# Gate and decay rows copied to all partitions by DMA, and the rotary embedding's turned halves read across partitions by VectorE, in a two-layer trunk kernel

## The reference, cut to what matters

```python
def _rotary(a, pos):                       # layer 0, on the retention's q and k
    ang = pos[:, None] * inv[None, :]      # inv: 64 frequencies
    cos, sin = jnp.cos(ang), jnp.sin(ang)
    a1, a2 = a[..., :half], a[..., half:]  # the halves of a head's 128 channels
    return jnp.concatenate([a1 * cos - a2 * sin, a1 * sin + a2 * cos], -1)

def _mlstm_step(carry, inp):               # layer 0
    b = jnp.cumsum(lf, axis=-1)
    logw = jnp.where(_causal(c), b[..., :, None] - b[..., None, :] + it[..., None, :], -jnp.inf)
    m_t = jnp.maximum(b + m[..., None], logw.max(-1))
    w = jnp.exp(logw - m_t[..., None])
    carry_scale = jnp.exp(b + m[..., None] - m_t)
    ...

def _gdn_step(S, inp):                     # layer 1
    gc = jnp.cumsum(g, axis=-1)
    G = gc[..., :, None] - gc[..., None, :]
    A = beta[..., :, None] * jnp.einsum('bhtd,bhsd->bhts', k, k) * dec_strict   # exp(G), masked
    o = jnp.exp(gc)[..., None] * jnp.einsum('bhtd,bhde->bhte', q, S) + ...
```

## Time and profile before

| | |
|---|---|
| median of 3 runs | 1496.48 us (1495.94 to 1501.11) |
| profiled execution, its own time | 1487.38 us |
| its span, first to last instruction | 1485.6 us |
| TensorE busy | 1404.6 us (95%) |
| VectorE busy | 996.4 us (67%) |
| ScalarE busy | 723.0 us (49%) |
| GpSimd busy | 256.8 us (17%) |
| mean granted TensorE clock | 0.969 of full speed |

### The profile page before, as it was taken

How to read it: one execution, slowest core, us unless ns; L and a number is a source line. 1 busy time by engine, 2 the same in 40 slices (tenths; PEclk the granted TensorE clock), 3 DMA queues, 4 the chain that set the end, 5 groups by cost and what they waited for, 6 DMA issues and landing times.

```text
span 1485.6 us, 18615 instructions
## 1 busy us (share of the span) xinstructions
PE 1404.6 (95%) x8014; PEld 1202.4 (81%) x8014; DVE 996.4 (67%) x948; ACT 723.0 (49%) x608; POOL 256.8 (17%) x166
## 2 busy tenths in 40 slices
PE   7999997999999989999998897999999999999994
PEld 6898886799999788997667566888888888888882
DVE  4533466654454578662866756878888888888886
ACT  3434312433333467311221434767777677677771
POOL 0110303000000001000421040000000004356771
PEclk9999998999999999999798987999999999999997
DMA  6532732646443133212245275999999993400003
GB/s 248 162 102 86 238 100 77 222 141 192 145 132 114 39 98 102 80 54 58 66 140 183 83 266 219 370 384 382 380 371 392 385 377 141 170 15 15 16 15 101
DMA packets 80890, 254.81 MB, mean 172 GB/s; under 512 B 11568, under 2 KB 47700, under 8 KB 68008
## 3 DMA queue, kind: packets, MB, share of 16 engines
q1 hardware_dynamic: 66008, 224.53, 41.7%
q0 software_dynamic: 14800, 29.10, 6.4%
HBM read 306.09 MB, written 16.70 MB: 217 GB/s over the span
## 4 chain that ended last, share of the span: by engine, by line
PE 77%; DVE 11%; DMA 5%; ACT 4%; issue 3%; POOL 0%; POOLq 0%; SPq 0%; DVEq 0%; ACTq 0%
PE PS L615 11%; PE PS L617 10%; PE PS L616 10%; PE PS L1321 7%; PE PS L1319 7%; PE PS L1324 7%; DMA u_raw<-in_w_moe 4%; PE PS L595 3%; PE PS L1342 3%; PE PS L1346 3%; PE PS L1343 3%; PE PS L1021 2%; ACT u_hi L1735 1%; PE PS L733 1%; PE PS L739 1%
## 5 line engine op out<-in xcount | busy, mean ns | idle before, releaser
L2598 DVE TENSOR_TENSOR u_lo<-u_raw,u_hi 128x2816 fp32r<-128x2816 f32 x144 | 442.9, 3090 | 106.8 <-ACT u_hi L1735 106.5
L1735 ACT ACTIVATE u_hi<-u_raw 128x2816 fp32r<-128x2816 f32 x144 | 368.1, 2562 | 163.9 <-DMA u_raw<-in_w_moe 113.6
L615 PE MATMUL PS<-x_in_hi,p_hi 128*128 128x304 f32 x480 | 155.5, 324 | 10.7 <-DVE x_in_lo L1978 10.7
L1319 PE MATMUL PS<-u_hi,xg_hi 128*128 128x512 f32 x576 | 141.6, 378 | 4.9 <-DVE xg_lo L2680 2.5
L617 PE MATMUL PS<-x_in_hi,p_lo 128*128 128x304 f32 x480 | 146.2, 305 | 0.0
L616 PE MATMUL PS<-x_in_lo,p_hi 128*128 128x304 f32 x480 | 146.2, 305 | 0.0
L1321 PE MATMUL PS<-u_hi,xg_lo 128*128 128x512 f32 x576 | 142.5, 380 | 0.0
L1924 POOL DMA_INDIRECT u_raw<-in_w_moe,wpick x48 | 125.4, 2612 | 90.5 <-PE PS L1324 66.4
L1324 PE MATMUL PS<-u_lo,xg_hi 128*128 128x512 f32 x576 | 140.9, 377 | 0.0
L615 PE MATMUL PS<-x_out_hi,w_parts 128*128 128x304 f32 x416 | 127.5, 306 | 7.0 <-DVE x_out_lo L1978 7.0
L617 PE MATMUL PS<-x_out_hi,w_parts 128*128 128x304 f32 x416 | 126.5, 304 | 0.0
(11 more groups left out here) (536 smaller groups left out, 2496.7 us busy)
## 6 DMA issues: line engine op xcount, KB each, us to landing
u_raw<-in_w_moe SPq DMA_DIRECT2D x96, 1408.0 KB, 8.3
p_raw<-in_w_first SPq DMA_DIRECT2D x40, 512.0 KB, 3.5
p_raw<-in_w_second SPq DMA_DIRECT2D x28, 512.0 KB, 3.5
dring<-in_ffn_w_down SPq DMA_DIRECT2D x8, 1408.0 KB, 7.4
wring<-in_ffn_w_gate SPq DMA_DIRECT2D x9, 1024.0 KB, 5.6
wring<-in_ffn_w_up SPq DMA_DIRECT2D x9, 1024.0 KB, 8.7
wring<-in_w_out SPq DMA_DIRECT2D x2, 2048.0 KB, 7.9
o_rows<-zT POOLq DMA_DIRECT2D x6, 512.0 KB, 6.8
```

What stands on the lines that cost most here:

```text
L615: mm(out, w[0], x[0], start=start, stop=False)
L1319: mm(PSf[:, a:a + w], x_hi, w_hi[:, a:a + w], start=k == 0, stop=False)
L1735: A(uhi[n % HIS][:], uraw[n % RAW][:], COPY).then_inc(s("u_hi"), 1)
L2598: TT(ulo[n % RAW][:], uraw[n % RAW][:], uhi[n % HIS][:].bitcast(F32), SUB).then_inc(s("u_lo"), 1)
```

## The change

**Rows.** The products `decays`, `carries` and those for `GROW[2]` and `GROW[0]` are gone. POOL stores the rows into a small DRAM tensor `row_copies`, waits for the store, and loads them back to all 128 partitions with a stride of zero: `ROW[4]` as three loads into the parts of `wm`, `ROW[6]` into `ebc`, `GROW[2]` into `qe` and `decI`, `GROW[0]` into `kb`, and the block ends into `dbc`. VectorE's `m_ex` now takes two heads in one instruction, from `wm` itself, and stands in iterations 9 and 10 in place of 7 and 8. ScalarE no longer copies `ebc`, and takes `exp` of `qe` in place. `decI` gets its mask with one addition.

**Rotary embedding.** `rotate` and its matrix are gone. `turn` is two VectorE instructions over 64 partitions each, in which the input comes from the other 64 partitions. POOL's `cos` multiply, which overwrites `turn`'s input, now waits for it (`rotm`). In POOL's program the store and the three loads of `ROW[4]` stand ahead of both multiplies, and the store of `ROW[6]` between them.

```diff
+        rowd = nc.dram_tensor("row_copies", [4, 4, 344], F32, kind="Internal").ap()
...
@@ TensorE, layer 0 @@
             for n in range(1, 6):
                 unit0(n)
-            rotate(0)
             unit0(6)
             pe.wait_ge(*at("ld_cc", 16))
+            unit0(7)
+            unit0(8)
+            unit0(9)
+            unit0(10)
             pe.wait_ge(*at("m_rows", 1))
-            decays(0, 4, at("m_rows", 1))
-            decays(1, 5, at("small_ev", 1))
-            unit0(7)
-            decays(2, 4, at("m_ex", 1))
-            decays(3, 5, at("m_ex", 2))
-            unit0(8)
             pe.wait_ge(*at("m_exp", 1))
-            carries(0, 4, at("m_ex", 3))
-            carries(1, 5, at("m_ex", 4))
-            unit0(9)
-            rotate(1)
-            carries(2, 4, at("m_ebc", 1))
-            carries(3, 5, at("m_ebc", 2))
-            unit0(10)
-            pe.wait_ge(*at("m_ebc", 3))
...
             unit0(12)
             pe.wait_ge(*at("a_ev", 12))
-            pe.wait_ge(*at("rotm", 2))
             pe.wait_ge(*at("m_col", 1))
-            pe.wait_ge(*at("m_ebc", 4))
+            pe.wait_ge(*at("small_ev", 1))
...
@@ TensorE, layer 1 @@
-                if n == 4:
-                    pe.wait_ge(*at("g_col", 1))
-                    pe.wait_ge(*at("small_ev", 2))
-                    for h in range(H):
-                        mm(PS[:, h, 0:315], row(h), GROW[2], start=True, stop=True)
-                    g_beta_rows([0, 1])
-                if n == 5:
-                    pe.wait_ge(*at("g_bcev", 1))
-                    g_beta_rows([2, 3])
                 if n == 6:
                     pe.wait_ge(*at("g_sqn", 1))
-                    pe.wait_ge(*at("g_eq", 1))
-                    pe.wait_ge(*at("g_dx", 4))
+                    pe.wait_ge(*at("g_col", 1))
...
@@ ScalarE @@
-                if n in (9, 10):
-                    carry(2 * n - 18, 4)
-                    carry(2 * n - 17, 5)
...
                 if n == 5:
                     tables()
-                    act.wait_ge(*at("g_bc", 1))
-                    A(dbc, PS[:, 0:4, T:T + 11], COPY)
-                    A(qe, bank4(0), EXP).then_inc(s("g_eq"), 1)
+                    act.wait_ge(*at("g_qd", 16))
+                    A(qe, qe, EXP).then_inc(s("g_eq"), 1)
...
@@ POOL @@
+            def copy_rows(slot, src, n, at_=0):
+
+                pool.dma_start(rowd[slot][:, at_:at_ + n], src).then_inc(s("row_st"), 16)
+
+            def spread_rows(dst, slot, a, n, signal):
+
+                pool.dma_start(dst, rowd[slot][:, a:a + n].unsqueeze(0).to_broadcast([128, 4, n])).then_inc(s(signal), 16)
+
+            pool.wait_ge(*at("m_rows", 1))
+            copy_rows(0, ROW[4][:, 0:T], T)
+            pool.wait_ge(*at("row_st", 16))
+            spread_rows(wm[:, :, 0:A1], 0, 0, A1, "m_md")
+            spread_rows(wm[:, :, A1:A2], 0, 128, A2 - A1, "m_md")
+            spread_rows(wm[:, :, A2:ATT], 0, 256, ATT - A2, "m_md")
             pool.wait_ge(*at("ld_c0", 16))
             cos = const(C0, "cos").rearrange("p (a b) -> p a b", a=2)
             for a in range(2):
-                pool.wait_ge(*at("rot", a + 1))
+                pool.wait_ge(*at("rotm", a + 1))
                 q = P[:, 4 * a:4 * a + 4, :]
                 G.tensor_tensor(q, q, cos[:, a:a + 1, :].to_broadcast([128, 4, T]), MUL).then_inc(s("ropec"), 1)
+                if a == 0:
+                    pool.wait_ge(*at("m_exp", 1))
+                    copy_rows(1, ROW[6], 344)
+            pool.wait_ge(*at("row_st", 32))
+            spread_rows(ebc, 1, 0, 344, "m_cd")
...
             for j, m in enumerate(ORDER1[n] for n in CONVS):
+                if j == 2:
+                    pool.wait_ge(*at("g_gc", 1))
+                    copy_rows(2, GROW[2][:, 0:T], T)
+                    copy_rows(3, GROW[0][:, 0:T], T)
+                    pool.wait_ge(*at("row_st", 64))
+                    spread_rows(qe, 2, 0, T, "g_qd")
+                    spread_rows(decI, 2, 0, T, "g_dd")
+                    spread_rows(kb, 3, 0, T, "g_kd")
+                if j == 4:
+                    pool.wait_ge(*at("g_rows", 1))
+                    copy_rows(2, GROW[2][:, T:T + 11], 11, T)
+                    pool.wait_ge(*at("row_st", 80))
+                    spread_rows(dbc, 2, T, 11, "g_ed")
                 pool.wait_ge(*at("cin", j + 1))
...
@@ VectorE @@
             def turn(a):
...
-                dve.wait_ge(*at("rot", a + 1))
-                TT(turned[a], bank4(0), sin[:, a:a + 1, :].to_broadcast([128, 4, T]), MUL).then_inc(s("rotm"), 1)
+                dve.wait_ge(*at("a_ev", 4 + 4 * a))
+                low, high, q = slice(0, 64), slice(64, 128), P[:, 4 * a:4 * a + 4, :]
+                STT(turned[a][low], q[high], -1.0, sin[high, a:a + 1, :].to_broadcast([64, 4, T]), MUL, MUL)
+                TT(turned[a][high], q[low], sin[low, a:a + 1, :].to_broadcast([64, 4, T]), MUL).then_inc(s("rotm"), 1)
...
-            def m_ex(h, b):
-                mask = const(C0, "mask")
+            def m_ex(c):
                 dve.wait_ge(*at("ld_c0", 16))
-                dve.wait_ge(*at("m_bc", h + 1))
-                TT(wm[:, h, 0:A1], mask[:, 0:A1], PS[:, b, 0:TP], SUB)
-                TT(wm[:, h, A1:A2], mask[:, A1:A2], PS[:, b, 128:TP], SUB)
-                TT(wm[0:R2, h, A2:ATT], mask[0:R2, A2:ATT], PS[0:R2, b, 256:T], SUB).then_inc(s("m_ex"), 1)
+                dve.wait_ge(*at("m_md", 48))
+                v = wm[:, 2 * c:2 * c + 2, :]
+                TT(v, const(C0, "mask").unsqueeze(1).to_broadcast([128, 2, ATT]), v, SUB).then_inc(s("m_ex"), 1)
...
-                if n == 7:
-                    m_ex(0, 4)
-                    m_ex(1, 5)
                 if n == 8:
                     turn_add(0)
-                    m_ex(2, 4)
-                    m_ex(3, 5)
+                if n in (9, 10):
+                    m_ex(n - 9)
                 if n == 10:
                     turn(1)
...
-                if n == 5:
-                    beta(0)
-                    dve.wait_ge(*at("g_eq", 1))
-                    for h in range(H):
-                        TT(decI[:, h, 0:256], PS[:, h, 0:256], incl[:, 0:256], ADD)
-                        TT(decI[0:R2, h, 256:T], PS[0:R2, h, 256:T], incl[0:R2, 256:T], ADD).then_inc(s("g_dx"), 1)
                 if n == 6:
-                    beta(1)
+                    dve.wait_ge(*at("g_dd", 16))
+                    TT(decI, decI, incl.unsqueeze(1).to_broadcast([128, H, T]), ADD).then_inc(s("g_dx"), 1)
                 if n == 8:
                     dve.wait_ge(*at("g_l2r", 1))
                     link(TT(P[:, 4:8, :], P[:, 4:8, :], sqn, MUL))
+                    dve.wait_ge(*at("g_kd", 16))
                     TT(kb, P[:, 4:8, :], kb, MUL).then_inc(s("g_kb"), 1)
...
```

More of the change, by code:

```diff
@@ L787, in ffn @@
                 ln_var("n0f_")
-            def rotate(half):
-                pe.wait_ge(*at("ld_c0", 16))
-                pe.wait_ge(*at("a_ev", 4 + 4 * half))
-                if half:
-                    pe.wait_ge(*at("rotm", 1))
-                for m in range(4):
-                    last = mm(PS[:, m, 0:T], const(C0, "rot"), P[:, 4 * half + m, :], start=True, stop=True)
-                last.then_inc(s("rot"), 1)
             def r_scores(h, bank, free):
@@ L824, in r_state @@
                 state_mm("r_", h, ktok, vd, vb[h % 2], slice(128 * h, 128 * h + 128), RPAIRS[h], 0)
-            def decays(h, bank, free):
-                pe.wait_ge(*free)
-                mm(PS[:, bank, 0:T], row(h), ROW[4][:, 0:T], start=True, stop=True).then_inc(s("m_bc"), 1)
-            def carries(h, bank, free):
-                pe.wait_ge(*free)
-                mm(PS[:, bank, 0:344], row(h), ROW[6], start=True, stop=True).then_inc(s("m_eb"), 1)
             def m_scores(h, bank, free):
@@ L992, in _ @@
             pe.wait_ge(*at("xlo", 8))
-            def g_beta_rows(heads):
-                for h in heads:
-                    last = mm(PS[:, 4 + h % 2, 0:T], row(h), GROW[0][:, 0:T], start=True, stop=True)
-                last.then_inc(s("g_bc"), 1)
             def g_scores(heads):
@@ L1433, in o_ev @@
                 A(xT[:, h, :], PS[:, bank, 0:T], COPY).then_inc(s("r_oev"), 1)
-            def carry(h, bank):
-                act.wait_ge(*at("m_eb", h + 1))
-                A(ebc[:, h, :], PS[:, bank, 0:344], COPY).then_inc(s("m_ebc"), 1)
             def weights(h):
                 act.wait_ge(*at("m_col", 1))
-                act.wait_ge(*at("m_ex", h + 1))
+                act.wait_ge(*at("m_ex", h // 2 + 1))
                 A(wm[:, h, 0:A1], wm[:, h, 0:A1], EXP, bias=mcol[:, h:h + 1])
@@ L2766, in put @@
         c[:v.shape[0], a:a + n] = v
-    rot = np.zeros((128, 128))
-    for j in range(64):
-        rot[64 + j, j] = -1.0
-        rot[j, 64 + j] = 1.0
-    put(c0, C0, "rot", rot)
     pos = np.concatenate([np.arange(TP), np.tile(2048 + np.arange(NS), NB)]).astype(f)
```

22 lines of the change are left out of this document (9 added, 13 removed), and 2 rows, old and new, of the table SHARED.

## The result

The changed kernel takes 1475.54 us (median of 4 executions, 1474.44 to 1477.41) against 1496.35 (4 of the kernel before): ratio 0.987, 95% interval 0.9838 to 0.9903. It is faster, as forecast; the gap is 20.8 us, and 1475.5 lies 2.5 us under the range of 1478 to 1490. The profiled execution took 1474.52 us, span 1472.7: 12.9 us under the profiled one of before, where the sum said 13.7.

What follows compares the result with a forecast made beforehand. TensorE, busy for 95% of the span, was taken as the bound; 10.26 + 4.75 - 1.3 = 13.7 us took the profiled 1487.38 to 1473.7, scaled to the runs' median as 1483 us, range 1478 to 1490.

Steps and rivals of the forecast that it cites:

- the sum: Whole kernel: 10.26 us from layer 0 plus 4.75 from layer 1 less a 1.3 stall, a gain of 13.7 us.
- 4.1 to 9.4: Layer-0 row copies: the spreads land 4.1 to 9.4 us after issue, the range of a 0.5 MB store.
- about 2.4: Layer 1: TensorE's idle time before kb's products was to remain about 2.4 us in the new profile.
- Rival 4: Row copies in both layers: 128 partitions reading the same DRAM serialize, making the kernel slower, 1505 us at 41 GB/s; chance 0.06.
- 4.75: Layer 1: ScalarE can evict unit 6 some 4.75 us earlier, taken as the gain there.
- so I count no lost clock: Layer 1: the stretch holding the 2.35 us idle time had mean granted clock 0.98, so nothing was subtracted.
- 4.86: Layer 1: TensorE time of the eight removed products, 4.86 us; ScalarE's chain was taken instead.
- The stall: Layer 0, before unit 9: POOL's cos multiply delays VectorE's split, so TensorE waits 1.3 us (bounds 0 and 4.5).
- rival 1: Layer 0: POOL's multiplies win both races against VectorE's splits; stall 3.0 us, gain 10.6, time 1486 us; chance 0.12.
- second race: Layer 0: POOL's second cos multiply starts before unit 13's split; m_col comes 3.4 us later, 1.4 of it not covered.
- 10.26: Layer 0: TensorE time saved by removing the eight rotate, four decay and four carry products, 10.26 us.
- the rotary part's 4.1 us: Layer 0: the eight removed rotate products, 2 x 2.05 us of TensorE, were to shorten the span by 4.1 us.

Runs made afterwards that it cites:

- e12: Changed kernel plus unread layer-1 products of the removed ones' columns, reading 128 rows of constants instead of 4 gate rows; 1477.92 us.
- e7: Changed kernel with the eight removed layer-1 products of the 4 gate rows issued again, their results unread; 1486.15 us.
- e15: Same edit as e7 on the changed kernel, run again beside e12; 1485.17 us.
- e4: Changed kernel with the 2.1 MB load of stA issued behind the load of unit 14 instead of unit 8; 1475.46 us.
- e8: Changed kernel with warm(8, 2), unread products of constants, ahead of TensorE's layer-1 wait for the gate rows; 1479.55 us, ratio 0.9898.
- e13: Changed kernel with the shorter fill warm(4, 2) ahead of TensorE's layer-1 wait for the gate rows; 1477.21 us, ratio 0.9906.
- e5: Changed kernel with GpSimd's first cos multiply ahead of the three spreads instead of behind them; 1478.16 us.
- e10: Kernel before, with only the fill warm(8, 2) ahead of TensorE's layer-1 wait for the gate rows; 1494.90 us, ratio 1.0016.
- e9: Changed kernel with both the stA load behind that of unit 14 and the layer-1 fill warm(8, 2); 1473.63 us, ratio 0.9863.
- e14: Changed kernel with both the stA load behind that of unit 14 and the layer-1 fill warm(4, 2); 1468.87 us, ratio 0.9861.
- e6: Changed kernel with GpSimd's first cos multiply made to wait for VectorE's split of unit 9; 1477.95 us.

## Why the prediction was right, and where it was wrong

**The direction and the mechanism were right.** No products between units 5 and 6; `turn` 2.84 us; the spreads landed 6.2 to 7.8 us after issue, within 4.1 to 9.4; `m_ex` waited for no DMA; the layer-1 copies cost nothing; the idle time before `kb`'s products is 1.9 us (about 2.4 said). Rival 4 is refuted: 0.95 MB read from one place landed within 9.4 us of the first issue, 100 GB/s, far from 49. That the profiled spans differ by 12.9 us where the sum said 13.7 is in part luck: the two changed stretches give 7.2 and 3.6, and 2.1 come from elsewhere, where the half-clock stretches of the two traces lie differently.

**The step that did most to put the result outside the range is the last one:** "The median of the runs is 1496.48, 0.6% above the profiled one; scaled, 1496.48 x 1473.7 / 1487.38 = 1482.7". It takes three runs and one execution for fixed values. Of 102 executions the median is 1493.4; the profiled 1487.4 is among the lowest tenth, and the three were all above the median. That was bad luck: of medians of four drawn from the 102 only 6 in 100 reach the 1496.35 of the first comparison. From 1493.4 the same 13.7 give 1479.7, and the range moved by as much, 1474.7 to 1486.7, would have held 1475.5. The measured 1475.5 is 1.8 under its own kernel's 16-execution median, so of the 7.5 us between forecast and result 3.3 are the first, 1.8 the second, and 2.4 are left to the size of the gain (16.1 for 13.7).

**Layer 1 was under-sized: 4.75 forecast, 3.6 between the first two profiles, 7.6 usually** (21.2 to 21.5 in five traces without a fill, to 13.7). The step was "so I count no lost clock". In the trace read, the removed products ran at full clock; in six of seven traces with them part of them or of what follows did not. The clock behind the idle time was left out of the sum as well. In the changed kernel's trace 5.9 us of work ran at half clock there (527.7 to 533.6), in the kernel before's 3.4. By an estimate, half of the difference, that is the 1.2 us which the 3.6 lacks to the forecast. Taking 4.86 for the products was not far off (3.8 by e12, with 128 rows), and e7 and e15 show that the products are the cause, not the shorter work on ScalarE and VectorE.

**The stall was under-sized: 1.3 forecast, 3.05 measured.** "so it runs from 44 to 47.4, over this split" had the right event, part of rival 1's (its 3.0 us), at the wrong time. The store landed after 5.6 us, not 3.4, because it shared the engines with `stA` (2.43 against 5.20 us of waiting, e4), the issues ended at 46.25, not 44, and the multiply's end moved to 49.14. Rival 1's second race was not lost: `m_col` cost TensorE nothing. The split starts in the record 0.5 us ahead of the multiply and still ends after it, so the rule quoted from the Trainium skill (SBUF — State Buffer, "SBUF: two separate sides") agrees in its price, a whole instruction, and not, by these starts, in who goes first.

The stall also costs clock, which the sum put at nothing. Eight traces have the changed kernel's layer 0 as it stands (three of it, e7, e8, e12, e13, e15), and in seven 3.4 or 6.8 us at half clock follow the stall; their transposes start at 65.4 to 67.4, not 64.33. This is the second of the three traces of the changed kernel:

```profile
66.04 1.47 PE L596 MATMUL PS<-cc,proj 128*128 128x128 f32 x12
```

Of all twenty traces ten have 1.25 to 3.3 us of idle time between 47 and 51 us, and in nine of them a half-clock stretch starts within 1.5 us of its end. The other ten, with 0 to 0.95 us, have none there. (e5's 1.45 us of idle time at 63 us has none.)

Layer 0 by the first two traces (10.26 - 3.05 = 7.2, the 7.2 of the transposes) and layer 1's 7.6 make 14.8, inside 14.3 to 17.9. With the median of the eight, 66.1, layer 0 gives only 5.4, and the two make 13.0. So 3.1 of the 16.1 us are not explained by the two stretches.

## What to carry to other kernels

Before a forecast in absolute time, ask for more executions than one: which stretches of the one trace ran at which clock says how lucky it was, and a gain of 1% is no larger than the kernel's own scatter. A removed product that brings TensorE forward is worth something only as far as the next load and the next split can follow: here 2.6 of the rotary part's 4.1 us and the clock after them went that way, until a 2.1 MB load whose data nobody wanted for some 45 us more was issued six units later. Over the whole kernel that showed as 1.5 us. Where TensorE must wait anyway, products that fit into the wait are worth trying; count their time from a trace first.

## What the runs showed of the hardware

- Eight products of 4 rows (4x315 and 4x304, fp32) had 6.8 us at half clock over or behind them in six of seven traces, also where TensorE had been busy until then (e10); the same columns with 128 rows of other values had not (e12, one trace).
- Behind 4.2 to 4.3 us of idle time all fifteen traces have 3.4 or 6.8 us at half clock; with products in it, four of five traces have none (e8, e9, e10, e14) and one 3.4 us (e13).
- VectorE reads the other 64 partitions at its usual pace, 1.42 us for 1216 elements, but 64 partitions take as long as 128.
- GpSimd's issues of DMAs beside a VectorE split cost it nothing that shows (e5, e6); its multiply made one take 4.38 us.
- A store of four rows of 1.2 KB took 5.6 us to land while 2.1 MB were under way, and 2.8 us without them (e4).
